# Order of the work between the output projections and the MLPs of a decoder trunk: weight rounding before tokens, mixed tokens' remainders on GpSimd, the root's table loaded earlier

## The reference, cut to what matters

```python
x = x + jnp.concatenate([mix, mem_out], axis=-1) @ p['w_out'][l]
h2 = rmsnorm(x, p['norm2'][l])
x = x + jnp.square(jax.nn.relu(h2 @ p['w_mlp1'][l])) @ p['w_mlp2'][l]
```

## Time and profile before

| | before |
|---|---|
| three executions, us | 1254.06, 1259.02, 1259.39 |
| median, us | 1259.02 |
| span of the profiled execution, us | 1251.9 |
| PE busy | 1177.3 us, 94% |
| DVE busy | 849.9 us, 68% |
| ACT busy | 516.0 us, 41% |
| POOL busy | 432.9 us, 35% |
| mean granted TensorE clock | 0.985 |

### The profile page before, as it was taken

How to read it: one execution, slowest core, us unless ns; L and a number is a source line. 1 busy time by engine, 2 the same in 40 slices (tenths; PEclk the granted TensorE clock), 3 DMA queues, 4 the chain that set the end, 5 groups by cost and what they waited for, 6 DMA issues and landing times.

```text
span 1251.9 us, 23862 instructions
## 1 busy us (share of the span) xinstructions
PE 1177.3 (94%) x9338; PEld 1124.8 (90%) x9338; DVE 849.9 (68%) x1332; ACT 516.0 (41%) x1013; POOL 432.9 (35%) x332
## 2 busy tenths in 40 slices
PE   6998998999999999999999998798999999999996
PEld 6877888899999999999899855697999999999996
DVE  7667568776776767556643887667967767677634
ACT  7445334443343434334422277534434434333321
POOL 3363014453443444221036210011634434444312
PEclk9999999999999999999999999999899999999997
DMA  7632321322323223423255276022223232232302
GB/s 286 215 119 67 132 85 51 118 85 99 104 68 118 85 75 118 146 68 102 96 146 138 94 261 243 1 84 61 94 87 113 72 118 85 69 117 85 103 33 72
DMA packets 46229, 134.96 MB, mean 108 GB/s; under 512 B 4178, under 2 KB 6354, under 8 KB 45490
## 3 DMA queue, kind: packets, MB, share of 16 engines
q1 hardware_dynamic: 45026, 125.39, 30.0%
q0 software_dynamic: 1104, 8.15, 2.1%
HBM read 123.15 MB, written 7.03 MB: 104 GB/s over the span
## 4 chain that ended last, share of the span: by engine, by line
PE 70%; DVE 13%; ACT 6%; POOL 5%; issue 3%; DMA 2%; SPq 0%; ACTq 0%; DVEq 0%; POOLq 0%
PE psum L640 30%; PE psum L622 23%; PE psum L556 11%; DVE weights_split L1400 3%; ACT weights_split L1021 2%; ACT squares L1033 1%; DVE inv_rms L1421 1%; DMA rotated<-keys 1%; DMA rotated<-projected 1%; DVE residual L1425 1%; POOL projected L2089 1%; POOL projected L2090 1%; PE psum L711 1%; POOL rotated L2088 1%; PE psum L806 1%
## 5 line engine op out<-in xcount | busy, mean ns | idle before, releaser
L640 PE MATMUL psum<-operand_b,weights_split 128*128 128x272 f32 x1536 | 196.8, 289 | 2.2 <-DVE weights_split L1489 1.9
L640 PE MATMUL psum<-operand_a,weights_split 128*128 128x272 f32 (+1 forms) x1536 | 196.6, 289 | 1.9 <-DVE weights_split L1489 1.9
L640 PEld LDWEIGHTS psum<-operand_b,weights_split 128*128 128x128 f32 x1536 | 195.1, 190 | 2.6 <-DVE weights_split L1489 2.2
L640 PEld LDWEIGHTS psum<-operand_a,weights_split 128*128 128x128 f32 x1536 | 195.0, 190 | 2.2 <-DVE weights_split L1489 2.2
L556 PE MATMUL psum<-operand_b,weights_split 128*128 128x272 f32 x1344 | 177.0, 292 | 6.3 <-DVE weights_split L1400 6.1
L556 PEld LDWEIGHTS psum<-operand_b,weights_split 128*128 128x128 f32 x1344 | 171.3, 190 | 12.2 <-DVE weights_split L1400 8.0
L556 PE MATMUL psum<-operand_a,weights_split 128*128 128x272 f32 (+1 forms) x948 | 128.4, 294 | 20.6 <-DVE weights_split L1400 16.6
L556 PEld LDWEIGHTS psum<-operand_a,weights_split 128*128 128x128 f32 x948 | 122.1, 193 | 27.3 <-issue 16.5
L1400 DVE TENSOR_TENSOR weights_split<-weights_raw,weights_split 128x1024 fp32r<-128x1024 f32 (+1 forms) x66 | 86.4, 1309 | 45.9 <-ACT weights_split L1021 45.9
L1971 POOL TENSOR_TENSOR mem_keys<-weights_raw 128x512 f32<-128x512 f32 x28 | 39.7, 1419 | 212.4 <-DMA weights_raw<-in_weights 212.4
L1021 ACT ACTIVATE weights_split<-weights_raw 128x1024 fp32r<-128x1024 f32 (+1 forms) x66 | 66.3, 1004 | 91.8 <-PE psum L556 90.6
(11 more groups left out here) (288 smaller groups left out, 2065.9 us busy)
## 6 DMA issues: line engine op xcount, KB each, us to landing
weights_raw<-in_weights SPq DMA_DIRECT2D x186, 512.0 KB, 3.7
cache_tiles<-in_page_k SPq DMA_DIRECT2D x16, 384.0 KB, 4.0
cache_tiles<-in_page_v SPq DMA_DIRECT2D x16, 384.0 KB, 4.1
cache_tiles<-in_mem_k SPq DMA_DIRECT2D x8, 512.0 KB, 4.5
cache_tiles<-in_mem_v SPq DMA_DIRECT2D x8, 512.0 KB, 5.1
residual<-in_x SPq DMA_DIRECT2D x1, 2176.0 KB, 12.8
rotated<-projected POOLq DMA_DIRECT2D x4, 408.0 KB, 7.2
rotated<-keys POOLq DMA_DIRECT2D x4, 408.0 KB, 7.0
```

Of the source, the lines that this page charges most:

```text
L640: mm = pe.matmul(ps[:, bank, 0:part.stop - part.start], w(wr), hidden[:, ar, 4 * (c % 2) + kk, part], start=(kk == 0 and wr == 0 and ar == 0),
```

## The change

In both layers' seams:

- ScalarE rounds the weights of the unit after next as soon as an out unit is done, and the tokens after it.
- ScalarE rounds mixed tokens 0, 1 and 2 behind the tokens of out units 5, 6 and 7, and number 3 as the first thing of the MLP.
- GpSimd takes the remainders of the mixed tokens: number 0 behind its sixth addition of squares less one (k = 5), number 1 behind k = 6, numbers 2 and 3 behind the last. VectorE has them no more.
- VectorE takes the remainder of MLP unit 2's weights before the inverse root, where it was behind unit 0's result.
- In the fourth plain unit, ScalarE squares the hidden tile before it rounds the weights of products 5 and 6, and VectorE takes the unit out before their remainders.

In layer 0 alone, ScalarE takes a root of one column before the out units, so that the table for roots is loaded there. `mixed_high` of before is now `pooled_high`; layer 1 has the same edits with its own names, and they are left out here.

```diff
@@ -1055,6 +1055,11 @@
+            def mixed_high(l, k):
+
+                act.wait_ge(tok_mixed, KQ * l + k + 1)
+                act.activation(mixed_tokens[:, :, 0, k, :], mixed_raw[:, :, 1, k, :], ACT.Copy).then_inc(tok_hi, 1)
+
@@ -1101,10 +1106,10 @@
                     if j == 0:
                         root(r)
+                    hidden_high(0, j // 2, j % 2)
                     if j == PLAIN - 1:
                         up_high(u0, 0, FIRST_DOWN, 5)
                         up_high(u0, 0, FIRST_DOWN, 6)
-                    hidden_high(0, j // 2, j % 2)
@@ -1127,9 +1132,7 @@
                 if l == 0:
                     act.wait_ge(pool_stored, 16)
-                for k in range(KQ):
-                    act.wait_ge(tok_mixed, KQ * l + k + 1)
-                    act.activation(mixed_tokens[:, :, 0, k, :], mixed_raw[:, :, 1, k, :], ACT.Copy).then_inc(tok_hi, 1)
+                mixed_high(l, KQ - 1)
                 for j in range(PLAIN):
                     plain(j)
@@ -1305,24 +1308,25 @@
             for j in range(2, MIXT):
                 high(U_POOL + j + HL)
-                mixed_high(j)
+                pooled_high(j)
+            own.step(act.activation(tiny[:, 13:14], epsc, ACT.Sqrt))
             for j in range(KT):
                 if j == KT - 1:
                     late_tokens(U_MLP0, B)
-                    high(U_OUT0 + j + HL)
+                high(U_OUT0 + j + HL)
                 residual_tokens(U_OUT0 + j, j, R_MLP0, A, A_raw)
-                if j < KT - 1:
-                    high(U_OUT0 + j + HL)
+                if j > KQ:
+                    mixed_high(0, j - KQ - 1)
             mlp(U_MLP0, B, R_MLP0, R_IN1, [(G_IN1, A)])
@@ -1501,25 +1505,18 @@
-                def tokens_rest(kk):
-                    dve.wait_ge(tok_hi, KQ * l + kk + 1)
-                    dve.tensor_tensor(mixed_tokens[:, :, 1, kk, :], mixed_raw[:, :, 1, kk, :],
-                                      mixed_tokens[:, :, 0, kk, :].bitcast(F32), ALU.subtract).then_inc(tok_lo, 1)
-
                 def plain(j):
                     if j == PLAIN - 1:
-                        for q in range(3, 7):
+                        for q in range(3, 5):
                             up_rest(u0, 0, FIRST_DOWN, q)
                     dve.wait_ge(unit_done, u0 + j + 1)
...
-                    if j + HL < PLAIN:
+                    if 0 < j < PLAIN - HL:
                         rest(u0 + j + HL)
-                        tokens_rest(2 * j)
-                        tokens_rest(2 * j + 1)
-                    for q in ((), (0,), (1, 2), ())[j]:
+                    for q in ((), (0,), (1, 2), (5, 6))[j]:
                         up_rest(u0, 0, FIRST_DOWN, q)
@@ -1570,6 +1567,7 @@
+                rest(u0 + HL)
                 inverse(r)
                 dve.wait_ge(rms_ready, r + 1)
@@ -1943,7 +1941,7 @@
-            def sum_squares(r, cols=TOK):
+            def sum_squares(r, cols=TOK, behind=None):
...
+                    if behind:
+                        behind(k)
+
+            def tokens_rest(l, kk):
+
+                pool.wait_ge(tok_hi, KQ * l + kk + 1)
+                pool.tensor_tensor(mixed_tokens[:, :, 1, kk, :], mixed_raw[:, :, 1, kk, :],
+                                   mixed_tokens[:, :, 0, kk, :].bitcast(F32), ALU.subtract).then_inc(tok_lo, 1)
@@ -2074,7 +2080,17 @@
-            sum_squares(R_MLP0)
+            def seam(l):
+
+                def behind(k):
+                    if k > KQ:
+                        tokens_rest(l, k - KQ - 1)
+                    if k == KT - 1:
+                        tokens_rest(l, KQ - 1)
+
+                return behind
+
+            sum_squares(R_MLP0, behind=seam(0))
             mlp(U_MLP0, B, R_IN1)
```

14 lines of the change are left out of this document (7 added, 7 removed).

## The result

| | before | changed |
|---|---|---|
| executions beside each other, us | 1253.0 to 1259.39, 5 runs | 1238.9 to 1241.47, 5 runs |
| median, us | 1254.35 | 1240.77 |
| span of the profiled execution, us | 1251.9 | 1237.1 |
| forecast, us | | 1247.1 (1241 to 1254) |

The ratio is 0.9876, with a 95% interval of 0.9859 to 0.9893: the change saves 1.1 to 1.4%, some 13.6 us by the medians (forecast 11.9).

A forecast was written before the change was run, and what follows sets the result against it. TensorE, with 70% of the chain of waits, was taken as the bound, waiting at two seams. Gains of 4.6 and 7.3 us, 11.9 together, took the span from 1251.9 to 1240.0; plus 7.1 gave 1247.1 us, range 1241 to 1254.

The forecast's parts named there:

- I keep the distance: Last step: the runs' median stays 7.1 us above the profiled span, so a new span of 1240.0 means 1247.1 us.
- The first seam's loss of 1.5 at M2: First seam, third MLP unit: starts 20.3 us after the first unit, before 18.72, through blocked VectorE work.
- Weights ahead of tokens: Out units: next weights ready sooner, gaining 4.2 us in the first seam and 7.4 in the second.
- Remainders on GpSimd: Four per seam, 1.97 us each, each blocking VectorE some 1.7 us; losses of 1.5 and 3.0 us by seam.
- The lock: VectorE operations with two SBUF inputs and GpSimd's exclude each other for a whole instruction; 1.1 us more behind one square sum.
- Root table early: First seam: the 1.28 us load leaves the chain, costed at nothing; without VectorE's cover worth up to 1.3 us.
- Order in the plain units: Third MLP unit to the first pair's fifth product: 21.2 us becomes 18.1, gaining 3.1 in each seam.
- What is late next: After the fifth product: product 5 waits 0.7 us, product 6 0.3, the down unit 1.9; losses 1.2 and 0.2.
- Clock: Rival, 0.14: TensorE's clock falls in the seams' new waits, 1.9 to 2.7 us a fall, giving 1250.9 to 1252.5.
- Copy misses: Rival, 0.08: ScalarE's copy is late, the first pair still stalls with slow clock, 9.6 us lost, giving 1256.7.
- Lock without effect: Rival, 0.07: GpSimd's remainders fall into gaps and hardly block VectorE, 21.6 us gained, giving 1237.4.
- Slower by GpSimd's price: Rival, 0.05: GpSimd's remainders cost far more; gain gone at 3.45 us each, 1271 us at 5.

The follow-up runs named there:

- run 3: Changed kernel, with GpSimd's four mixed-token remainders begun only once VectorE has done MLP unit 2's weights; 1235.58 us, ratio 0.9857.
- experiments 2: Changed kernel with the mixed tokens' remainders back on VectorE, in the first plain units; 1235.5 us, ratio 0.9857.
- run 9: Changed kernel with GpSimd's mixed-token remainders behind unit 2's weights and without the early root table; 1236.11 us, one execution.
- experiment 4: Changed kernel with the old order of the fourth plain unit on both ScalarE and VectorE; 1239.64 us, ratio 0.9888.
- 7: Changed kernel with GpSimd's mixed-token remainders behind unit 2's weights and the old order of the fourth plain unit; 1236.09 us, ratio 0.9855.
- run 10: Changed kernel with the mixed tokens' remainders back on VectorE and the old order of the fourth plain unit; 1233.86 us, ratio 0.9841.
- run 1: Kernel before with one edit, ScalarE rounding weights ahead of tokens in the out units of both seams; 1238.66 us, ratio 0.9879.
- 12: Run 8 with the mixed tokens' remainders on VectorE; 1237.85 us, ratio 0.9876.
- run 8: Changed kernel, GpSimd's mixed-token remainders behind unit 1's weights, VectorE's unit 2 weights and the fourth plain unit's order as before; 1231.91 us, ratio 0.9822.
- 5: Changed kernel measured once more, beside the kernel before; 1239.87 us, ratio 0.9879.
- 6: Changed kernel without the early load of the root's table; 1240.69 us, ratio 0.989.
- 11: Run 8 with the changed kernel's order of the fourth plain unit put back; 1235.17 us, ratio 0.9852.

## Why the prediction was right or wrong

**The step that failed is the last: "I keep the distance".** The seams were forecast at 11.9 us and gave 13.46. But the forecast set them against a median of 1259.02, 7.1 us above the profiled span. That was a median of three, two of which lay at 1259. The five sessions of this study put the same kernel at 1253.45 to 1254.5 (the first among them with the three known runs and two more), and every run of which the span is known is about 1.8 us above it. The profiled execution of before was worth 1253.7 us, and the forecast on that base would have been 1241.8, 1.0 from what came. So 5.3 of the 6.3 us are the base. That two of three runs lay so high was bad luck; to take their distance from one profiled span for a property of the kernel was the error. In the sum itself each seam was forecast 0.3 us too long at M2 and 0.6 behind P4. (The first seam's loss of 1.5 at M2 is 20.3 − 18.72 = 1.6, which makes the sum 11.8.)

**Weights ahead of tokens: right, and worth more than its term.** 4.2 and 7.4 us were forecast for the out units, 4.20 and 7.36 measured. The 1.25 us that the edit also gives before M2 was in no term: the forecast reckoned unit 2's start from the chain of blocked items alone, where it hides.

**Remainders on GpSimd: right in price and mechanism.** The length alone was an estimate of 1.97 us, between ends of 1.6 and 2.3. Undisturbed it is 1.94 to 1.95 (run 3, least and median of eight); in the changed kernel, where VectorE's operations are in its way too, 2.14 to 2.92:

```profile
L1960 POOL TENSOR_TENSOR mixed_tokens<-mixed_tokens_raw,mixed_tokens x8: 2142/2283/2921, 173.3 to 855.6; 128x816 fp32r<-128x816 f32 x8
```

The blocked operations of VectorE came nearly as forecast (its E is M0 here): 2.07 and 1.83 us where 0.44 and 0.72 are normal, and the two weight remainders 5.83 together (1.7 + 1.2 and 2.9 forecast). Unit 2 started at E + 20.02 (forecast 20.3). The waits of TensorE were 1.36, 2.12, 0.94 and 1.65 us against 1.7, 2.3, 1.4 and 1.8; the second of them is not new, for the kernel before waited 2.12 us for its last tile as well. What was wrong is the credit given for it. The trade was thought nearly neutral, as the fourth plain unit's gain paid for it; experiments 2 and 3 show that the place chosen costs 4.5 us at M2 and some 2.4 per seam in the end.

**The lock.** VectorE's addition of two SBUF tensors took 0.71 us alone (195.67 in the changed kernel) and 1.81 beside a remainder of GpSimd (run 9). The reciprocal, with one input, took 3.55 us beside the four remainders in runs 3 and 9, as it did without them. The Trainium skill (SBUF — State Buffer, "SBUF: two separate sides") has the lock for a VectorE operation with two SBUF inputs against one of GpSimd that reads SBUF, held for the whole instruction; these rows agree.

**Root table early: right.** Nothing in this kernel (20.02 us with and without it). "Without that cover it would be worth up to 1.3" was too small at M2: 1.98 in run 9, since the late root walks into the lock; by the next pair it is 0.67.

**Order in the plain units: right number, wrong reason.** 18.17 us were measured for 18.1, but experiment 4 has 18.20 without the new order. The agreement is luck. P4 wanted its bank 38.2 us after M0 because M2 was late, and the copy needs 35.3 to 35.8 in runs 2, 3, 7 and 10. The wait went since TensorE came later, and the kernel paid for that at M2. The old lateness (38.68 and 37.28 in run 1) is not VectorE's remainders as such, as the prediction had it: run 10 has them there and stands at 35.8. It takes both, remainders on VectorE and unit 2's weights behind the root (runs 1 and 12); either one moved away is enough (10, and 8, where P4 starts at 35.59 without a wait).

**What is late next: right place, mis-sized.** The down unit waited 1.32 and 1.35 us, not 1.9, and product 5 0.24, not 0.7. That is 0.6 us per seam. In the first seam the pair's last weight subtraction ended at E + 38.0 and not 38.6, and the addition 12.9 us behind it and not 13.3; why was not tested.

**The rivals.** *Clock*: a fall did come, in the second seam, behind tile 7's wait of 2.12 us (19 matmuls in 3.20), and the same wait in the first seam brought none. It cost nothing: M0 to M2 is 20.02 us in both, since TensorE had waits there that the slow matmuls filled. Two windows (us, PE, PEld, DVE, ACT and POOL busy, granted clock, DMA share, GB/s):

```profile
190.00:194.00 4.00, 3.02 (x18) 2.51 (x19) 4.00 (x2) 1.66 (x2) 4.00 (x2) 1.00 0.02 4
...
854.00:857.00 3.00, 3.00 (x11) 2.13 (x12) 3.00 (x2) 1.11 (x2) 3.00 (x2) 0.60 0.00 0
```

*Copy misses*: no. The copy ended 0.52 us before P4 (218.15 + 0.37 against 219.04), not 0.1; with the old order in experiment 4 it was 0.14. So what the order did bring is 0.4 us of margin. *Lock without effect*: no. *Slower by GpSimd's price*: no, 1.94 us undisturbed and 2.92 at most, against the 3.45 from which the gain would be gone.

## What to carry to other kernels

Price a change against a time that belongs to the profiled execution: a profile's span and a median of few runs can differ by more than the change is worth. When work goes to GpSimd, ask first what two-input operations of VectorE on the path will stand beside it; the same eight subtractions cost 4.5 to 5 us ahead of them (changed kernel against 2 and 3, both seams together) and saved 4 to 6 behind them (12 against 8). But run 10, which leaves them on VectorE and has unit 2's weights ahead of the root, can't be told from 8. And a wait that disappears may only mean that TensorE arrives later: undo the part that is credited with it before the credit is booked.

## What the runs showed that was not expected

The clock behind a wait is a matter of the execution. Behind the last wait of 1.95 us, the same in all kernels, the 192 matmuls took about 25.85 us in the profiles of the kernel before and of runs 1, 2, 3, 5, 6, 7, 9, 10, 11 and 12, and about 24.3 in those of the changed kernel and of runs 4 and 8. So 1.5 us of a difference between two profiled spans can be this alone, more if a fall in a seam is added, and a part worth less has to be read from the stages of the trace that the clock did not touch. The same wait of 2.44 us went both ways inside run 8. What decides it stays open; no run was made for it.
